# The rows between two transformer layers: transposes over four tiles into one bank per eighth of the columns, and the norm's weight and bias folded into what follows

## The reference

```python
x = _layer_norm(DEEPNORM_ALPHA * x + g_a * y, ln1_g[l], ln1_b[l])
x = _layer_norm(DEEPNORM_ALPHA * x + g_m * _squared_relu_mlp(x * (1 + sc_m) + sh_m, mlp_w1[l], mlp_w2[l]),
                ln2_g[l], ln2_b[l])
# next layer
h = x * (1 + sc_a) + sh_a
hc = ctx * (1 + csc_a) + csh_a
...
x = _layer_norm(DEEPNORM_ALPHA * x + g_a * y, ln1_g[l], ln1_b[l])
```

## Time and profile before

| what | us |
|---|---|
| median of 3 runs | 2991.48 |
| lowest, highest | 2990.63, 2997.6 |
| the profiled execution | 2992.68 |
| its span, first to last instruction | 2990.9 |
| TensorE busy (94% of the span) | 2801.1 |
| VectorE busy (46%) | 1363.7 |
| ScalarE busy (29%) | 877.5 |
| GpSimd busy (18%) | 550.6 |

### The profile page before, as it was taken

How to read it: one execution, slowest core, us unless ns; L and a number is a source line. 1 busy time by engine, 2 the same in 40 slices (tenths; PEclk the granted TensorE clock), 3 DMA queues, 4 the chain that set the end, 5 groups by cost and what they waited for, 6 DMA issues and landing times. The chain is left out here.

```text
span 2990.9 us, 40569 instructions
## 1 busy us (share of the span) xinstructions
PE 2801.1 (94%) x15614; PEld 2295.7 (77%) x15614; DVE 1363.7 (46%) x2161; ACT 877.5 (29%) x1684; POOL 550.6 (18%) x375
## 2 busy tenths in 40 slices
PE   6998994999999999999957999999799999999998
PEld 3666784788888888888846888888677888888886
DVE  3575436573333333333374555555555333333336
ACT  4243324341121121121124434334443212211222
POOL 0000002242112121121140000000025223323321
PEclk7999997999999999999978999999999999999999
DMA  6574225441011011010042111110256111111112
GB/s 251 183 307 156 74 65 184 141 127 57 28 42 42 28 45 39 28 56 28 28 141 81 45 36 39 47 36 8 74 152 190 43 46 52 56 42 42 56 42 57
DMA packets 192673, 238.95 MB, mean 80 GB/s; under 512 B 15992, under 2 KB 153840, under 8 KB 186416
## 3 DMA queue, kind: packets, MB, share of 16 engines
q1 hardware_dynamic: 192272, 237.30, 24.7%
q10 hardware_dynamic: 288, 0.10, 0.0%
HBM read 203.72 MB, written 37.88 MB: 81 GB/s over the span
## 5 line engine op out<-in xcount | busy, mean ns | idle before, releaser
L2156 DVE TENSOR_TENSOR y<-y,pair 128x1024 f32<-128x1024 f32 x280 | 341.6, 1220 | 334.6 <-PE pair L2290 334.5
L2288 PE MATMUL pair<-m_wbh,m_ath 128*128 128x512 f32 x1120 | 437.1, 390 | 4.2 <-DVE y L2156 3.0
L2290 PE MATMUL pair<-m_wbh,m_atl 128*128 128x512 f32 x1120 | 437.8, 391 | 0.0
L2289 PE MATMUL pair<-m_wbl,m_ath 128*128 128x512 f32 x1120 | 436.8, 390 | 0.0
L2210 DVE TENSOR_TENSOR m_atl<-m_sq,m_ath 128x512 fp32r<-128x512 f32 x156 | 100.7, 647 | 646.5 <-POOL m_sq L2061 646.5
L2015 ACT ACTIVATE m_rel<-pair 128x512 f32<-128x512 f32 x160 | 88.9, 556 | 983.6 <-PE pair L2314 973.0
L2061 POOL TENSOR_TENSOR m_sq<-m_rel 128x512 f32<-128x512 f32 x160 | 155.5, 972 | 1125.2 <-ACT m_rel L2015 1125.1
L2314 PE MATMUL pair<-hth,m0n_wal 128*128 128x512 f32 (+1 forms) x768 | 272.2, 354 | 0.0
L2313 PE MATMUL pair<-htl,m0n_wah 128*128 128x512 f32 (+1 forms) x768 | 272.1, 354 | 0.0
L2312 PE MATMUL pair<-hth,m0n_wah 128*128 128x512 f32 (+1 forms) x768 | 271.6, 354 | 0.0
L2288 PEld LDWEIGHTS pair<-m_wbh,m_ath 128*128 128x128 f32 x1120 | 210.4, 188 | 50.3 <-DVE y L2156 4.7
(11 more groups left out here) (273 smaller groups left out, 5229.2 us busy)
## 6 DMA issues: line engine op xcount, KB each, us to landing
a_ring<-in_w_mod SPq DMA_DIRECT2D x40, 1024.0 KB, 9.3
m_rawb<-in_mlp_w SPq DMA_DIRECT2D x64, 512.0 KB, 4.3
m_rawa<-in_mlp_w SPq DMA_DIRECT2D x60, 512.0 KB, 4.1
x_rows<-r_res SPq DMA_DIRECT2D x28, 512.0 KB, 5.1
r_raw<-cat_cols SPq DMA_DIRECT2D x18, 512.0 KB, 6.4
mod_w<-in_w_mod SPq DMA_DIRECT2D x8, 1024.0 KB, 12.3
r_xin<-in_x SPq DMA_DIRECT2D x16, 512.0 KB, 4.4
gate_pre<-a0g_gout SPq DMA_DIRECT2D x20, 256.0 KB, 2.0
```

What stands on the lines that cost most here:

```text
L2156: dve.tensor_tensor(k.y[:, t, :], k.y[:, t, :], k.pair[t % 2][:, :], ALU.add).then_inc(s_y, 1)
L2288: pe.matmul(o, ath[:, m, ts], bh[:, m, cols], start=m == 0, stop=False)
L2289: pe.matmul(o, ath[:, m, ts], bl[:, m, cols], start=False, stop=False)
L2290: i = pe.matmul(o, atl[:, m, ts], bh[:, m, cols], start=False, stop=m == M - 1)
```

## The change

`stage_rows(0, 2)` is replaced by `stage_between`. Four things differ.

- The tile is only normalised, in one pass (`normalise`); the norm's weight `g` and bias `b` are not applied to the rows. For the modulated input they go into the modulation: `scale = scale * g`, `shift = shift + scale * b`, on vectors of 128x16 (`lnr`, `lnc`, `lnt`); `g` and `b` come as 16 rows of 128, loaded at the end of layer 0's block and turned by TensorE.
- The transposes of up to four tiles (512, 512 and 256 tokens) go into one bank for each of the eight column groups `kt`. ScalarE modulates 128x512 in one pass. The conversion to `hth` is VectorE's at even steps and ScalarE's at odd ones; `htl` is VectorE's.
- Only the eight image tiles are stored in `x_dram`, and without `g` and `b`.
- So layer 1's block applies them to the residual: two more VectorE passes over `xres` in each tile, ahead of the wait for `s_yps`, with two more broadcast rows, in 128 x 8 x 128 layout, in the columns of `hth` that hold the context. They are loaded between the gate rows and `x` of tile 0, and VectorE's and GpSimd's wait for the rows becomes 96 instead of 64.

The diff, without declarations:

```diff
+def stage_between(nc, io, k):
...
+    groups = groups_of(TOK)
+    steps = [(a, n, kt) for a, n in groups for kt in range(KT)]
+    by_act = lambda i: i % 2 == 1
+    later = {g * KT + 2 * i: t for g, (a, n) in enumerate(groups[1:]) for i, t in enumerate(range(a // P, (a + n) // P))}
...
+            for t in range(XT):
+                sp.wait_ge(s_norm, t + 1)
+                sp.dma_start(rows(k.x_dram, t, False), res[:, t, :]).then_inc(s_store, 16)
+            sp.wait_ge(s_store, 16 * XT)
+        @block.scalar
+        def _(act):
+            act.activation(rstd[:, 0, :], k.mv[:, 0:T, 1], ACT.Sqrt, bias=k.eps[:, 0:1]).then_inc(s_std, 1)
+            act.wait_ge(s_fold, 4)
+            for i, (a, n, kt) in enumerate(steps):
+                col = lambda part: k.mod[:, 1, part * KT + kt, a // SEQ:a // SEQ + 1]
+                act.wait_ge(s_tr, i + 1)
+                if i >= NB:
+                    act.wait_ge(s_hl, i - NB + 1)
+                act.activation(modt[:, i % NB, 0:n], k.bank[kt][:, 0:n], ACT.Identity, scale=col(SC_A), bias=col(SH_A)).then_inc(s_mod, 1)
+                if by_act(i):
+                    act.wait_ge(s_mod, i + 1)
+                    act.activation(placed(k.hth, kt, a, n), in_rows(modt[:, i % NB, :], a, n), ACT.Copy).then_inc(s_ha, 1)
+        @block.vector
+        def _(dve):
+            k.clear_last(dve)
+            def normalise(t):
+                dve.tensor_scalar(res[:, t, :], y[:, t, :], k.mv[:, t, 0:1], rstd[:, 1, t:t + 1], ALU.subtract, ALU.mult).then_inc(s_norm, 1)
+            dve.wait_ge(s_std, 1)
+            dve.reciprocal(rstd[:, 1, :], rstd[:, 0, :]).then_inc(s_rec, 1)
+            dve.wait_ge(s_rec, 1)
+            for t in range(2):
+                normalise(t)
+            scale, shift = [k.mod[:, 1, part * KT:(part + 1) * KT, :] for part in (SC_A, SH_A)]
...
+            dve.tensor_tensor(lnt[:, :, :], scale, column(1), ALU.mult).then_inc(s_fold, 1)
+            dve.wait_ge(s_fold, 2)
+            dve.tensor_tensor(shift, shift, lnt[:, :, :], ALU.add).then_inc(s_fold, 1)
+            dve.tensor_tensor(scale, scale, column(0), ALU.mult).then_inc(s_fold, 1)
+            for t in range(2, 4):
+                normalise(t)
+            for i, (a, n, kt) in enumerate(steps):
+                hi, v = placed(k.hth, kt, a, n), in_rows(modt[:, i % NB, :], a, n)
+                dve.wait_ge(s_mod, i + 1)
+                if by_act(i):
+                    dve.wait_ge(s_ha, i // 2 + 1)
+                else:
+                    dve.tensor_copy(hi, v).then_inc(s_hd, 1)
+                    dve.wait_ge(s_hd, i // 2 + 1)
+                dve.tensor_tensor(placed(k.htl, kt, a, n), v, f32(hi), ALU.subtract).then_inc(s_hl, 1)
+                if i in later:
+                    normalise(later[i])
+        @block.tensor
+        def _(pe):
+            pe.wait_ge(s_lnr, 32)
+            pe.transpose(k.bank[7][:, 0:2 * KT], lnr[:, :], k.ident[0:2 * KT, 0:2 * KT]).then_inc(s_lnt, 1)
+            for g, (a, n) in enumerate(groups):
+                tiles = range(a // P, (a + n) // P)
+                def turn(t, kt):
+                    pe.wait_ge(s_norm, t + 1)
+                    if g:
+                        pe.wait_ge(s_mod, KT * (g - 1) + kt + 1)
+                    elif kt == KT - 1:
+                        pe.wait_ge(s_fold, 1)
+                    at = (t - tiles[0]) * P
+                    i = pe.transpose(k.bank[kt][:, at:at + P], res[:, t, kt * P:(kt + 1) * P], k.ident[:, :])
+                    if t == tiles[-1]:
+                        i.then_inc(s_tr, 1)
+                if g == 0:
+                    for t in tiles:
+                        for kt in range(KT):
+                            turn(t, kt)
+                else:
+                    for kt in range(KT):
+                        for t in tiles:
+                            turn(t, kt)
...
     if final:
+        over = nc.alloc_sbuf_tensor_at(f"{rtag}_over", [P, KT, TOK], F32, offset=BASE)
+        past = [over[:, :, SEQ + i * P:SEQ + (i + 1) * P] for i in range(2)]
...
+            if final:
+                for x, name in zip(past, ("ln2_g", "ln2_b")):
+                    sp.dma_start(x, bass.AP(tensor=io[name].tensor, offset=(layer - 1) * D, ap=[[0, P], [P, KT], [1, P]])).then_inc(s_row, 16)
             residual_in(0)
             for t in range(tiles):
                 if t + 2 < tiles:
...
+            if not final:
+                for i, name in enumerate(("ln2_g", "ln2_b")):
+                    sp.dma_start(k.ahead["ln2"][0][i * KT:(i + 1) * KT, :], io[name][layer].rearrange("(k p) -> k p", p=P)).then_inc(k.ahead["ln2"][1], 16)
...
+            pool.wait_ge(s_row, 96 if final else 64)
...
+            dve.wait_ge(s_row, 96 if final else 64)
...
+                if final:
+                    x = xres[:, 0, :].rearrange("p (j q) -> p j q", q=P)
+                    dve.wait_ge(s_xr, 16 * (t + 1))
+                    dve.tensor_tensor(x, x, past[0], ALU.mult).then_inc(s_past, 1)
+                    dve.wait_ge(s_past, 2 * t + 1)
+                    dve.tensor_tensor(x, x, past[1], ALU.add).then_inc(s_past, 1)
+                    dve.wait_ge(s_past, 2 * t + 2)
                 if t >= 2:
                     dve.wait_ge(s_store[t % 2], 16 * (t // 2))
                     dve.wait_ge(s_tr, t - 1)
...
-              (stage_rows, (0, 2)), (stage_attention, ()), (stage_block, (1,))]
+              (stage_between, ()), (stage_attention, ()), (stage_block, (1,))]
     for stage, args in stages:
         stage(nc, io, k, *args)
         k.end_stage()
```

More of the change, by code:

```diff
@@ L1349, in _, with placed, in_rows @@
                     turn(2 * m - 1)
+def stage_between(nc, io, k):
+    y = k.y
+    sb = Place(nc, "r02", k.after_y)
+    T = XT + CT
+    NB = 4
+    res = sb("res", [P, T, D])
+    modt = sb("modt", [P, NB, 512])
+    rstd = sb("rstd", [P, 2, T])
+    lnc, lnt = sb("lnc", [P, 2, KT]), sb("lnt", [P, KT, 2])
+    lnr, s_lnr = k.ahead["ln2"]
+    place = Place(nc, "a1", k.after_ht)
+    ahead = {x: (place(f"raw{x}", [P, KT, P]), k.early(f"a1_raw_{x}")) for x in "kqv"}
+    assert place.at <= k.y_at and sb.at <= END - 536
+    k.ahead["kqv"] = ahead
+    sem = lambda n: k.sem(f"r02_{n}")
+    s_std, s_rec, s_norm, s_lnt, s_fold, s_tr, s_mod, s_ha, s_hd, s_hl = [
+        sem(x) for x in ("std", "rec", "norm", "lnt", "fold", "tr", "mod", "ha", "hd", "hl")]
+    s_store = sem("store")
+    groups = groups_of(TOK)
+    steps = [(a, n, kt) for a, n in groups for kt in range(KT)]
+    by_act = lambda i: i % 2 == 1
+    later = {g * KT + 2 * i: t for g, (a, n) in enumerate(groups[1:]) for i, t in enumerate(range(a // P, (a + n) // P))}
+    def placed(x, kt, a, n):
+        if a >= SEQ:
+            return x[:, kt, a:a + n]
+        r = a // GRID_W
+        return x[:, kt, 0:SEQ].rearrange("p (b r c) -> p r b c", r=GRID_R, c=BLK)[:, r:r + n // GRID_W, :, :]
+    def in_rows(x, a, n):
+        x = x[:, 0:n]
+        return x if a >= SEQ else x.rearrange("p (r b c) -> p r b c", b=GRID_W // BLK, c=BLK)
+    with nc.Block() as block:
+        @block.sync
+        def _(sp):
+            for x in "kqv":
+                col = "qkv".index(x) * D
+                sp.dma_start(ahead[x][0][:, :, :], io["c_w_in"][0].rearrange("(k p) n -> p k n", p=P)[:, :, col:col + P]).then_inc(ahead[x][1], 16)
+            for t in range(XT):
[26 more added lines that the diff above has]
+            scale, shift = [k.mod[:, 1, part * KT:(part + 1) * KT, :] for part in (SC_A, SH_A)]
+            column = lambda i: lnc[:, i, :].unsqueeze(2).broadcast_to([P, KT, 2])
+            dve.wait_ge(s_lnt, 1)
+            dve.tensor_copy(lnc[:, :, :].rearrange("p i j -> p (i j)"), k.bank[7][:, 0:2 * KT]).then_inc(s_fold, 1)
+            dve.wait_ge(s_fold, 1)
+            dve.tensor_tensor(lnt[:, :, :], scale, column(1), ALU.mult).then_inc(s_fold, 1)
[39 more added lines that the diff above has]
+                            turn(t, kt)
@@ L1777, in stage_block @@
     rsem = lambda n: k.sem(f"{rtag}_{n}")
-    s_row, s_xr = rsem("rows"), rsem("x")
+    s_row, s_xr, s_past = rsem("rows"), rsem("x"), rsem("past")
     s_raw = [rsem(f"raw{i}") for i in range(2)]
@@ L1802, in stage_block @@
     final = layer == DEPTH - 1
+    if not final:
+        k.ahead["ln2"] = nc.alloc_sbuf_tensor_at("r02_lnr", [2 * KT, P], F32, offset=END - 536), k.early("r02_lnr")
+        assert sb.at <= END - 536
     if final:
+        over = nc.alloc_sbuf_tensor_at(f"{rtag}_over", [P, KT, TOK], F32, offset=BASE)
+        past = [over[:, :, SEQ + i * P:SEQ + (i + 1) * P] for i in range(2)]
         growt, lng2, lnb2 = k.y[:, XT, :], k.y[:, XT + 1, :], sb("lnb2", [P, D])
@@ L2034, in _ @@
         def _(pool):
-            pool.wait_ge(s_row, 64)
+            pool.wait_ge(s_row, 96 if final else 64)
             for t in range(tiles):
@@ L2113, in fold @@
                 dve.tensor_tensor(scale, scale, column(0), ALU.mult).then_inc(s_fold, 1)
-            dve.wait_ge(s_row, 64)
```

(1 more changed line is left out.)

## The result

| | before | after |
|---|---|---|
| median, us | 2991.48 (15 runs) | 3002.0 (15 runs) |
| lowest to highest | 2988.04 to 2997.6 | 2997.16 to 3007.43 |
| the profiled execution | 2992.68 | 2998.85 |

The ratio is 1.0032, with a 95% interval of 1.0026 to 1.0039: 0.32% or 9.6 us slower (10.5 by the medians), little, but the interval leaves out no change. Of all runs in this document one, of e11_before_order, took 3222.99 us at a granted clock of 0.83 instead of 0.97; it is left out. The profiled execution of after lies 3.2 us under its median, that of before 1.2 over its own, so the two traces are only 6.0 us of span apart. The trace answers where the time is, the medians how much it is.

The account below looks back on a forecast made before the run. TensorE, busy 94% of the span, was taken as the bound, except in the stage between the layers, set by ScalarE. The terms -14.2 + 8.2 + 16.5 = +10.5 gave 3002.0 us; range 2983 to 3007, the forecast's own 2998 to 3007.

Parts of the forecast that it names:

- ahead of the stage, and the attention: Layer 0's MLP and the attention before and after the stage between the layers: no change, 0 us.
- stage between: Stage between the layers: would end near 1582.4 instead of 1596.6, 14.2 us saved, bounds 12.6 to 17.
- tile 0: Layer 1's projection, first tile: two more loads 4.4, two passes 2.45, gate product 1.3, together 8.2 us more TensorE wait.
- tiles 2 to 7: Layer 1's projection: VectorE's added passes alternate with GpSimd on the port, TensorE waits, 16.5 us more, bounds 0 to 20.
- after the projection: MLP loops behind layer 1's projection: no change, since TensorE's own instructions there are the same.
- The start and the clears: Start of the stage between: 71 clears at 0.083 us hide the dropped loads; dropping them is worth 0, VectorE starts 1550.5.
- The pair of steps: New stage, an even and an odd column step: VectorE takes 2.4 to 2.65 us a pair, ScalarE 2.1.
- the chain of a tile: Layer 1's projection, from one normalisation's end to the next through GpSimd and VectorE turns: 14.3 us, TensorE needing 11.8.
- the 4.2 at the end: End of layer 1's projection: VectorE's way to tile 7's normalisation stretches from 6.8 to 11 us, 4.2 more wait.
- (c): Rival, layer 1's projection: x comes ahead of GpSimd each time, tiles 12.8 to 13.4, +4 in all, 2995.5 us; chance 0.12.
- (a): Rival: loads hidden in the old time, passes fit ahead of GpSimd, so -10.4, 2981 us, faster; chance 0.08.
- (b): Rival, layer 1's projection: tile 0 pays its 8.2, but the passes don't delay the other tiles, 2985.5 us; chance 0.20.

Follow-up runs that it names:

- e11_before_order: The kernel before with tile 0's x and gate row loaded ahead of GpSimd's rows in both layers, and GpSimd's layer 1 passes in halves: 2986.63 us, ratio 0.998.
- e1: The changed kernel without the two row loads, the wait for them and the two passes over x, so the new stage alone: 2977.72 us, ratio 0.9948.
- e10: The kernel before with only the row loads, wait and two passes in layer 1's projection added, old stage kept: 3014.29 us, ratio 1.0076.
- e6: The changed kernel with the 72 semaphore clears at the start of the stage between the layers on GpSimd instead of VectorE: 2996.86 us, ratio 1.0012.
- e2: The changed kernel with the two row loads and their wait, but without the two passes over x: 2979.45 us, ratio 0.9954.
- e9: The changed kernel with GpSimd's multiply and add of layer 1's projection each cut into two instructions of 512 columns: 2992.03 us, ratio 0.9996.
- e3: The changed kernel with GpSimd's multiply and add of layer 1's projection done on 16 of 1024 columns: 2986.13 us, ratio 0.9978.
- e8: e7 with GpSimd's multiply and add of layer 1's projection each cut into two instructions of 512 columns: 2968.29 us, ratio 0.992.
- e7: The changed kernel with x loaded and passed a tile ahead, passes behind the low-half subtraction, x(0) before the gate row, clears on GpSimd: 2974.46 us, ratio 0.9939.

## Why the prediction was right

The forecast was 3002.0, and the median is 3002.0. The mechanism was right, term by term: the saved stage, the later tile 0, the turns between VectorE and GpSimd. That the two numbers agree to the last digit is luck: in the traces the terms add up to +6.0 and not to +10.5, and the profiled execution of after lies 3.2 under its median. By the times of e1 and e10 the halves of the change are -15.6 and +22.7, where -14.2 and +24.7 were forecast.

| term | predicted | measured |
|---|---|---|
| ahead of the stage, and the attention | 0 | -1.0 |
| stage between | -14.2 | -14.7 in the trace, -15.6 (11.7 to 19.2) by e1 |
| tile 0 | +8.2 | +8.3, and 1.4 behind it |
| tiles 2 to 7 | +16.5 | +12.8, and 0.9 to the first MLP product |
| after the projection | 0 | -1.8 |

- **The start and the clears.** Right. VectorE starts 6.1 after the square root with the loads gone, the trace has the clears in just that time, and e6 shows that they are what it stood behind.
- **The new stage.** From the square root to the attention's first own matmul it took 56.0 us and takes 41.3: 14.7 less. The forecast's own terms give 13.6 saved and not 14.2: for columns 512 to 1023 they are 1.2 + 2 x 2.4 + 2 x 2.1, which ends at 1577.4 and not at 1576.8. The clock that it took for the first transposes was about right: 32 of them took 5.38 us, between 7.9 at half clock and 4.4 at full (four times 1.97 and 1.09 of the earlier trace rows). The pair of steps is at the low end of the forecast (2.39 of 2.4 to 2.65), since the cast into the scattered output takes 0.42 to 0.43. By the Trainium skill (VectorE: DVE Perf Modes, Mode 2×_2P), which asks nothing of contiguity, it is the cheap one, and the trace agrees with 0.42: the dear one was put at 0.6. Against it 0.65 us were lost at the warming matmuls (4.61 instead of the 3.96 of the earlier trace rows).
- **Tile 0.** The start of the projection to the transposes of tile 0 took 35.5 us and takes 43.8. That this meets the 8.2 is in part luck, since two misses cancel. The loads cost 3.7 in e2 and 3.7 in after (x lands 15.8 after the first row's issue, 12.1 in the earlier trace rows), not 4.4. From x's landing to the transposes it is 8.06 instead of 4.21: 3.85, as predicted (3.75). The last 0.7 lies ahead of all this: the first row is issued 19.85 after the start of the projection, 19.12 in before; that place varies from 19.1 to 21.1 between the runs. TensorE's wait rose by 7.5 and not by 8.2. Missed too were the matmuls at half clock behind the longer wait: the transposes of tile 1 come 14.7 behind those of tile 0, 13.3 before. It isn't a fixed price: in e9 and e10, with waits of 12.9, that distance is 13.5.
- **The tiles.** The mechanism is as written, the chain of a tile predicted at 14.3 and measured at 14.27 (2238.31 - 2224.04). e3 and e9 show that the turns with GpSimd make it: without GpSimd's work a tile takes 11.8, with GpSimd's passes in halves 13.0. The sum of 16.5 was too large by 3.7, of which 2.3 is a slip: the five tiles at 2.3 and the 4.2 at the end count one tile twice, since there are six gaps between the seven transposes, and the last gap is the end. The rest is in the sizes. Tile 2 paid 0.1 instead of 0.8, tiles 3 to 5 paid 2.5 each instead of 2.3, and in tile 6 x came ahead of GpSimd, so that it paid 1.0. That is rival (c), for one tile in after, two in e10, and three in e6, whose projection is the same and took 82.4 us for the stretch where after took 82.5. What spreads the runs of after over 10 us stays open.
- **Behind it.** The forecast had the MLP unchanged. All of the 1.8 less lies ahead of TensorE's first product into `y`. Its wait there is 0.38 instead of 1.20, which is 0.8. The other 1.0 is the clock: the 48 matmuls ahead of that wait take 12.81 us now at a granted clock of 0.87, and took 13.81 at 0.80.
- **The rivals.** (a) falls with e2 and e10: the loads were not hidden and the passes didn't fit. (b) falls at tile 3, where TensorE waits 2.26. (c) came for one to three tiles of a run and not each time. The Trainium skill's rule (SBUF — State Buffer, SBUF: two separate sides), that one of the two engines holds the shared port for a whole instruction, now has its own test, and the runs agree: halving GpSimd's instruction takes VectorE's pass from 3.3 to 2.2 us, and 6 us (e8 against e7) to 10 us (e9 against after) off the time.

## What to carry to other kernels

Idle time of an engine is not room: VectorE waited 2.7 to 4.4 us a tile, and yet 2.45 of new work cost up to 2.5 us a tile, because it met GpSimd's two-input passes. Look at what the other engine does in that very window, lay its passes and yours out as one queue, and if they must overlap, cut the less urgent engine's instructions. And before a saving is believed or a load blamed, count the clears ahead of an engine's first work.

## What the runs showed of the hardware

- A semaphore clear on VectorE costs 0.080 to 0.086 us, and 72 of them were 5.8 us of VectorE's start; on the idle GpSimd of e6 they held up nothing that the trace shows. The page of the profile doesn't count them as busy; the trace has them under their line, L95.
- GpSimd pays the turns too: its pass of 1024 columns takes 2.40 alone and 3.26 when it has let VectorE go ahead.
- Cutting GpSimd's passes was nearly free: two of 512 columns take 2.52 us where one of 1024 takes 2.40 (last tile, alone: the row below is of e8).

```profile
2251.19 2.52 POOL L2187 TENSOR_TENSOR r_res<-r_res,r_lng 128x512 f32<-128x512 f32 x2 [3.30 <-PE pair L2416]
```
